# Dealing the later modulation blocks 12 and 8, instead of 10 and 10, to the two attention stages of a two-layer trunk step

## The chip, the core and the metric

The kernel runs on one core of a Trainium2 chip. It is measured in device microseconds of one launch. Before the change the median of three runs is 1972.08 us (1971.47 to 1976.73). About 0.3% (5.9 us) is what a measurement of this kernel can tell from no change.

## What is computed

One step of a two-layer trunk over 128 context tokens and 512 latent tokens of width 1024 (640 tokens in all). Each layer first computes its modulation, six vectors of 1024 for each of two conditions (context and latent), from the conditioning vector and a large matrix. Layer 0 mixes tokens with two kinds of attention, layer 1 with two kinds of recurrence, and each layer ends in a gated convolutional FFN.

```python
def trunk_layer(h, cond, p, mixer, ctx):
    sh1, sc1, g1, sh2, sc2, g2 = jnp.split(jax.nn.silu(cond) @ p['ada_w'] + p['ada_b'], 6, axis=-1)
    hn = rmsnorm(h, p['norm1']) * (1.0 + sc1) + sh1
    m, ctx_out = mixer(hn, p['mix'], ctx)
    h = h + g1 * m
    hn = rmsnorm(h, p['norm2']) * (1.0 + sc2) + sh2
    h = h + g2 * conv_ffn(hn, p)
    return h, ctx_out
...
def one(qblk):
    s = jnp.einsum('bhqd,bhkd->bhqk', qblk, k).astype(jnp.float32) * scale
    p = jax.nn.softmax(s, axis=-1).astype(v.dtype)
    return jnp.einsum('bhqk,bhkd->bhqd', p, v)
```

`ada_w` is 1024 x 6144 in each layer. The differential attention (A) takes two softmax maps per head and query block and subtracts one from the other; the latent attention (B) takes one. Both have four heads. Latent queries see 640 keys, context queries 128.

## The kernel before

All large weights go through one ring of two slots in SBUF. The SyncE queue issues the loads in the order of a list of blocks; a load into a slot waits until the block that lay there two places earlier is released by the matmuls that read it (`released`). A modulation block is 512 columns of `ada_w`, 2048 KB. There are 24 of them, numbered 0 to 23: blocks 0 to 3 (`ADA_FIRST = 4`) are computed at the very start, since layer 0 needs them at once. The other twenty are computed inside the two attention stages, ten in each (`BATCH = 10`): the first stage (A, g = 0) takes blocks 4 to 13 and the second (B, g = 1) blocks 14 to 23.

An attention stage has 20 units, numbered 0 to 19 here: four heads by five query blocks, the fifth of each head being the context queries (units 4, 9, 14, 19, with 128 keys only). In round u, TensorE works through this order (`att_pe`): the scores of unit u; half a modulation block (`products(u)`, so one block in two units); in the rounds of later heads the product of an earlier head's weights with its values (a round with u % 5 == 2 has both a latent and a context product); in the second stage's first five rounds the factor of the sub-norm (`sub_factor`); and the five transposes of unit u-1's probabilities. VectorE takes the maximum and scales the probabilities, ScalarE takes the exponential and copies the transposes out of PSUM. In the first stage the scores of unit u wait for the two exponentials of unit u-1 (`att0_exp`), since both maps share two PSUM places. The transposes of unit u-1 wait for its scaled probabilities (`att0_probs`, `att1_probs`).

The first half of a block begins with a wait for its load (`next_block`: `block_loaded0` or `block_loaded1`, one for each slot), and its second half releases the slot. Everything behind that wait in TensorE's queue waits too. Half a block is four matmuls of a 128 x 32 stationary operand against 128 x 512 columns, each placed in its own 32 output rows of one PSUM bank (the profile shows two records for each, so 8 for a half block). The stationary operand is a window into a row of zeros with the two conditioning columns in it, moved by two columns per block, so that all blocks of a batch add up in one bank. At the end of the stage the bank is copied once, turned (`batch_turn`) and added to the bias (`batch_take_cols`).

Just ahead of the first stage both slots are not alike. Block 4 is loaded long before, but block 5 goes into the slot that the last block of the input projection held until that projection ended. Behind block 23 in the list come the two blocks of the output projection.

Of the kernel before, what the change touches and what calls it, by code (L numbers as in the profile page):

```python
# [19 lines left out]
P = 128  # L20
# [16 lines left out]
EPS = 1e-6  # L37
ADA_FIRST = 4
RING = 2
BATCH = (24 - ADA_FIRST) // 2  # L40
COND0 = 2 * (BATCH - 1)
SLOT = 4096
SEG = ((0, NL), (NL, NT))
# [30 lines left out]
def build(nc, t_in, t_out):  # L74
# [3 lines left out]
    with ctx:  # L78
# [3 lines left out]
        def sem(name):  # L82
            return ctx.enter_context(nc.semaphore(name))
# [3 lines left out]
        def bank(b, n=512, p0=0, p1=P):  # L87
            return ps_all[p0:p1, 512 * b:512 * b + n]
# [49 lines left out]
        def pc(name, i=0, w=1, p0=0, p1=P):  # L138
            return par[p0:p1, PC[name] + i:PC[name] + i + w]
# [54 lines left out]
        def sg(name):  # L194
            if name not in S:
                S[name] = sem(name)
            return S[name]
# [27 lines left out]
        def mm(pe, out, lhsT, rhs, first=True, last=True):  # L225
            return pe.matmul(out, lhsT, rhs, start=first, stop=last)  # L226
# [36 lines left out]
        ada_row = lambda n: stat[:, 512 * (n % 2):512 * (n % 2) + 512]  # L263
        cond = lambda k, b: cond_b[:, COND0 + 32 * k - 2 * b:COND0 + 32 * k - 2 * b + 32]
        group_sum = small[:, 130:130 + 2 * BATCH]
        ada_w = {}

        def ada_products(pe, n, ks):

            g, b = divmod(n - ADA_FIRST, BATCH) if n >= ADA_FIRST else (None, 0)  # L270
            if ks[0] == 0:
                ada_w[n] = next_block(pe)
                if g is not None and b == 0:
                    pe.wait_ge(sg("ada_taken"), ADA_FIRST + g)
            for k in ks:
                p0 = 32 * (k % 4)
                ins = mm(pe, bank(ada_rows_bank(n), 512, p0, p0 + 32), cond(k, b), ada_w[n][:, k, :],
                         k < 4 and b == 0, k >= 4 and b == (0 if g is None else BATCH - 1))
            if ks[-1] == KT - 1:
                ins.then_inc(sg("ada_rows"), 1)  # L280
                released.append((sg("ada_rows"), n + 1))
# [18 lines left out]
                .then_inc(sg("ada_taken"), 1)  # L300

        def batch_take_rows(dve, g):
            dve.wait_ge(sg("ada_rows"), ADA_FIRST + BATCH * (g + 1))
            dve.tensor_copy(ada_row(g), bank(7)).then_inc(sg("ada_rowed"), 1)

        def batch_turn(pe, g):
            pe.wait_ge(sg("ada_rowed"), ADA_FIRST + g + 1)
            for m in range(4):
                ins = mm(pe, bank(7)[:, 32 * m:32 * m + 2 * BATCH], ada_row(g)[:, P * m:P * m + P], group_sum)
            ins.then_inc(sg("ada_cols"), 1)  # L310

        def batch_take_cols(dve, g):

            dve.wait_ge(sg("ada_cols"), ADA_FIRST + g + 1)
            n0 = ADA_FIRST + BATCH * g
            for l in range(2):
                a, b = max(n0, 12 * l), min(n0 + BATCH, 12 * l + 12)
                if a < b:
                    ins = dve.tensor_tensor(
                        mods[:, 8 * a:8 * b].rearrange("p (b m c) -> p b m c", m=4, c=2),  # L320
                        bank(7, P).rearrange("p (m b c) -> p b m c", m=4, c=2)[:, a - n0:b - n0],
                        pc(f"ada_b{l}", 4 * (a - 12 * l), 4 * (b - a)).rearrange("p (b m) -> p b m", m=4).unsqueeze(3)
                        .to_broadcast([P, b - a, 4, 2]), ALU.add)
            ins.then_inc(sg("ada_taken"), 1)
# [959 lines left out]
        def att_units():  # L1284
            return [(hd, qt) for hd in range(4) for qt in range(5)]
# [3 lines left out]
        ROUNDS = 21  # L1289

        latent_at = lambda hd: 2 * hd + 2 if hd < 3 else 7
        context_at = lambda hd: 2 * hd + 1 if hd < 3 else 8

        def att_pe(pe, g):
            maps = 2 - g
            units = att_units()
            x = f"att{g}_"

            def scores(u):
                if u >= len(units):
                    return
                hd, qt = units[u]
                if g == 1 and u < 2:
                    pe.wait_ge(sg("m0_copied"), U0_AT + 11 + u)
                if g == 0:
                    sides = ((0, 0, 64), (1, 64, P))
                    if u >= 1:
                        pe.wait_ge(sg(x + "exp"), 2 * u)  # L1310
                else:
                    sides = ((u % 2, 0, QK),)
                    if u >= 2:
                        pe.wait_ge(sg(x + "exp"), u - 1)
                lhs = lambda p0, p1: q_b[p0:p1, NT * hd + P * qt:NT * hd + P * qt + P]
                key = lambda p0, p1, a, b: k_b[p0:p1, NK * hd + a:NK * hd + b]
                if qt < 4:
                    for pair, p0, p1 in sides:
                        mm(pe, pair_ap(pair, 0, 512), lhs(p0, p1), key(p0, p1, 0, 512))
                    for pair, p0, p1 in sides:  # L1320
                        mm(pe, pair_ap(pair, 512, 640), lhs(p0, p1), key(p0, p1, 512, 640)).then_inc(sg(x + "scores"), 1)
                else:
                    for pair, p0, p1 in sides:
                        mm(pe, pair_ap(pair, 0, P), lhs(p0, p1), key(p0, p1, KP0, NK)).then_inc(sg(x + "scores"), 1)

            def transposes(u):
                if not 0 <= u < len(units):
                    return
                hd, qt = units[u]
                pe.wait_ge(sg(x + "probs"), u + 1)  # L1330
                if u >= 1:
                    pe.wait_ge(sg(x + "turned_out"), u)
                if u >= 6:
                    pe.wait_ge(sg(x + "out"), context_at((u - 1) // 5 - 1))
                pb = pr_b[:, (u % 2) * 2 * NT:(u % 2) * 2 * NT + NT]
                for kt in range(5 if qt < 4 else 1):
                    ins = pe.transpose(bank(4)[:, P * kt:P * kt + P] if kt < 4 else bank(5, P), pb[:, P * kt:P * kt + P],  # L1337
                                       ident[:, :])
                ins.then_inc(sg(x + "turned"), 1)

            def value(hd, kt):
                if kt == 0:
                    pe.wait_ge(sg(x + "turned_out"), 5 * hd + 4)
                    if hd >= 1:
                        pe.wait_ge(sg(x + "out"), latent_at(hd - 1))
                    elif g == 1:
                        pe.wait_ge(sg("sub_scaled"), 5)
                ins = mm(pe, bank(6), v_b[:, 512 * kt + P * hd:512 * kt + P * hd + P],
                         dT_b[:, (hd % 2) * 2560 + 512 * kt:(hd % 2) * 2560 + 512 * kt + 512], kt == 0, kt == 4)
                if kt == 4:  # L1350
                    ins.then_inc(sg(x + "values"), 1)

            def context_value(hd):
                pe.wait_ge(sg(x + "turned_out"), min(5 * hd + 6, 20))
                mm(pe, bank(5)[:, P:2 * P], v_b[:, 512 * 5 + P * hd:512 * 5 + P * hd + P],
                   dTp_b[:, (hd % 2) * P:(hd % 2) * P + P]).then_inc(sg(x + "values"), 1)

            def products(u):
                if 0 <= u < len(units):
                    if g == 1 and u == 0:  # L1360
                        pe.wait_ge(sg("head_root"), 1)
                    ada_products(pe, ADA_FIRST + BATCH * g + u // 2, range(4 * (u % 2), 4 * (u % 2) + 4))

            for u in range(ROUNDS):
                hd, r = u // 5 - 1, u % 5
                scores(u)
                products(u)
                if hd >= 0 and r == 2:
                    context_value(hd)
                if 0 <= hd < 3 and r > 0:  # L1370
                    value(hd, r)
                if g == 1 and hd < 0:
                    sub_factor(pe, r)
                if g == 0 and u == len(units):
                    up0_query(pe, 2)
                    up0_query(pe, 0)
                transposes(u - 1)
                if 0 <= hd < 3 and r == 0:
                    value(hd, 0)
            for kt in range(5):  # L1380
                value(3, kt)
            context_value(3)
# [80 lines left out]
        def att_dve(dve, g, ch):  # L1463
# [58 lines left out]
            if g == 1:  # L1522
                batch_take_cols(dve, 1)
# [804 lines left out]
        for piece in wkv_order():  # L2328
            piece_use[piece] = []
            for _ in range(banks_of.get(piece[0], 0)):  # L2330
                u = len(use_bank)
                b = FIRST_BANKS[u] if u < first_uses else 4 + (u - first_uses) % 3
# [1001 lines left out]
```

## Time and profile before

| | before |
|---|---|
| median of three runs | 1972.08 us (1971.47 to 1976.73) |
| the profiled execution's own time | 1973.24 us |
| its span in the profile | 1971.5 us |
| TensorE matmul busy | 1890.9 us (96%) |
| VectorE, ScalarE, GpSimd busy | 1094.3, 727.9, 139.5 us |
| DMA | 164.20 MB, mean 83 GB/s |
| first attention stage, about | 165 to 252 us |
| second attention stage, about | 268 to 343 us |

The span is one execution of the whole program. Each engine has its own row of busy time; a wait on an engine that is not the one everything else waits for costs nothing. TensorE is the engine to look at here, and the question at each place is whether it works, waits for another engine or waits for a load.

### The profile page before, as it was taken

To read this page: it belongs to the slowest core of one execution; us is meant where nothing else is said; L and a number is where in the kernel's file an instruction comes from. 1 tells how busy PE (TensorE), PEld (TensorE's weight loads), DVE (VectorE), ACT (ScalarE), POOL (GpSimd) and SP (SyncE) were. 2 spreads that over 40 slices of the span, in tenths; PEclk is the share of its full clock that TensorE was granted. 3 is DMA by queue.
4 is the path that set the end of the run, shared out by engine and by line. 5 is a ranking of instruction groups with operands and counts; after the bars stand their busy time and mean duration, and the time that the engine had idled before them with its cause. 6 is when DMAs were issued, how large, how long until landed. Compare 5 with 4: busy or idle time off the path is not lost.

```text
span 1971.5 us, 41405 instructions
## 1 busy us (share of the span) xinstructions
PE 1890.9 (96%) x18391; PEld 1693.8 (86%) x18391; DVE 1094.3 (56%) x2007; ACT 727.9 (37%) x1331; POOL 139.5 (7%) x137
## 2 busy tenths in 40 slices
PE   5998999999999999999999889898999999999997
PEld 2794444999999999999998678788779999999997
DVE  3646744575555562254565766766677554557223
ACT  2324565343332341132245644444324332334211
POOL 2000000000000000000002523322000000000000
PEclk8999999999999999999999899999999999999999
DMA  9125748121222222322221000000212122212322
GB/s 344 56 86 195 275 144 295 43 86 63 67 86 86 70 62 60 89 83 86 64 65 42 7 3 4 4 4 4 92 43 77 53 86 86 83 46 63 86 74 69
DMA packets 142034, 164.20 MB, mean 83 GB/s; under 512 B 2496, under 2 KB 107120, under 8 KB 141856
## 3 DMA queue, kind: packets, MB, share of 16 engines
q1 hardware_dynamic: 138736, 150.29, 23.7%
q0 software_dynamic: 3120, 11.26, 1.6%
q8 instruction: 145, 2.38, 0.5%
q14 instruction: 33, 0.27, 0.0%
HBM read 157.79 MB, written 3.75 MB: 82 GB/s over the span
## 4 chain that ended last, share of the span: by engine, by line
PE 87%; DVE 7%; ACT 2%; POOL 1%; issue 1%; DMA 1%; POOLq 0%; DVEq 0%; SPq 0%; ACTq 0%
PE ps L226 81%; DMA ring<-in_ada_w 1%; PE ps L2485 1%; POOL work L2849 1%; PE ps L1337 1%; DVE work L498 1%; DVE ring L2734 1%; DVE small L1473 1%; PE ps L2090 1%; ACT work L1401 0%; POOL work L2851 0%; PE ps L2463 0%; DVE x_lo_r L504 0%; PE ps L347 0%; PE ps L462 0%
## 5 line engine op out<-in xcount | busy, mean ns | idle before, releaser
L226 PE MATMUL ps<-x_hi_r,w_lo 128*128 128x320 f32 (+2 forms) x2224 | 516.1, 307 | 0.4 <-DVE w_lo L1702 0.4
L226 PE MATMUL ps<-x_hi_r,w_hi 128*128 128x320 f32 (+2 forms) x1792 | 428.7, 311 | 0.9 <-issue 0.9
L226 PE MATMUL ps<-x_lo_r,w_hi 128*128 128x320 f32 (+2 forms) x1792 | 424.8, 308 | 0.0
L226 PEld LDWEIGHTS ps<-x_hi_r,w_lo 128*128 128x128 f32 x2224 | 370.3, 187 | 1.8 <-issue 0.5
L226 PEld LDWEIGHTS ps<-x_lo_r,w_hi 128*128 128x128 f32 x1792 | 305.6, 188 | 0.0
L226 PEld LDWEIGHTS ps<-x_hi_r,w_hi 128*128 128x128 f32 x1792 | 303.8, 188 | 1.4 <-issue 1.3
L226 PE MATMUL ps<-work 64*64 64x64 f32 (+10 forms) x3284 | 269.4, 277 | 18.9 <-ACT work L1401 7.6
L226 PEld LDWEIGHTS ps<-work 64*64 64x64 f32 (+5 forms) x3284 | 173.1, 152 | 93.3 <-issue 59.0
L741 DVE SCALAR_TENSOR_TENSOR work<-ps,par,work 128x511 f32<-128x511 f32 (+1 forms) x188 | 103.4, 550 | 254.8 <-ACT work L908 244.8
L908 ACT ACTIVATE work<-ps,par 128x640 f32<-128x640 f32 x88 | 77.8, 884 | 374.3 <-PE ps L226 374.3
L785 ACT ACTIVATE w_hi<-ring 128x1024 fp32r<-128x1024 f32 (+1 forms) x152 | 135.6, 937 | 206.4 <-DMA ring<-in_ffn_down 183.3
L796 DVE TENSOR_TENSOR w_lo<-ring,w_hi 128x1024 fp32r<-128x1024 f32 (+1 forms) x152 | 158.5, 1077 | 88.9 <-ACT w_hi L785 88.9
L226 PE MATMUL ps<-g_lo,w_hi 128*128 128x320 f32 (+2 forms) x704 | 174.7, 309 | 0.0
L226 PE MATMUL ps<-work,ring 64*64 64x64 f32 (+3 forms) x2368 | 122.1, 238 | 8.1 <-DVE work L2752 4.0
L226 PEld LDWEIGHTS ps<-work,ring 64*64 64x64 f32 (+2 forms) x2368 | 95.0, 142 | 31.7 <-issue 25.9
L226 PEld LDWEIGHTS ps<-g_lo,w_hi 128*128 128x128 f32 x704 | 121.3, 188 | 0.0
L226 PE MATMUL ps<-x_lo_r,w_lo 128*128 128x320 f32 (+2 forms) x416 | 108.2, 310 | 0.0
L743 DVE SCALAR_TENSOR_TENSOR work<-ps,par,work 128x511 f32<-128x511 f32 (+1 forms) x188 | 103.3, 550 | 6.7
L448 DVE SCALAR_TENSOR_TENSOR h<-ps,mods,h 128x512 f32<-128x512 f32 (+2 forms) x76 | 34.8, 493 | 122.0 <-PE ps L226 121.8
L226 PE MATMUL ps<-x_hi_r,w_in_hi 128*128 128x320 f32 (+1 forms) x384 | 88.3, 312 | 0.5 <-issue 0.4
L226 PE MATMUL ps<-x_lo_r,w_in_hi 128*128 128x320 f32 (+1 forms) x384 | 86.8, 307 | 0.0
L226 PE MATMUL ps<-ring,cond 128*32 128x512 f32 x384 | 56.0, 667 | 18.0 <-DMA ring<-in_ada_w 18.0
(407 smaller groups left out, 2591.1 us busy)
## 6 DMA issues: line engine op xcount, KB each, us to landing
ring<-in_ada_w SPq DMA_DIRECT2D x24, 2048.0 KB, 8.2
ring<-in_ffn_up SPq DMA_DIRECT2D x44, 1024.0 KB, 7.7
ring<-in_ffn_down SPq DMA_DIRECT2D x16, 1408.0 KB, 6.9
ring<-in_l_w_in SPq DMA_DIRECT2D x11, 1024.0 KB, 5.2
ring<-in_l_w_out SPq DMA_DIRECT2D x4, 2048.0 KB, 8.5
ring<-in_l_w_in SPq DMA_DIRECT2D x3, 2048.0 KB, 9.7
h<-in_xT POOLq DMA_DIRECT2D x1, 2560.0 KB, 14.8
out_yT<-work POOLq DMA_DIRECT2D x2, 768.0 KB, 4.0
```

The costliest lines, as they stand in the source:

```text
L226: return pe.matmul(out, lhsT, rhs, start=first, stop=last)
L448: ins = dve.scalar_tensor_tensor(h(m, x, y), psum(u % 2, x, y), gate(m, c), h(m, x, y), ALU.mult, ALU.add)
L498: ins = dve.scalar_tensor_tensor(hn(t, x, y), h(t, x, y), gain(t, c), bank(6 + p)[:, x - a:y - a], ALU.mult, ALU.mult)
L741: ch(dve.scalar_tensor_tensor(acc(a + 1, b), psrc(a, b - 1), w0, acc(a + 1, b), ALU.mult, ALU.add))
L743: ins = dve.scalar_tensor_tensor(acc(a, b - 1), psrc(a + 1, b), w2, acc(a, b - 1), ALU.mult, ALU.add)
L785: act.activation(wh_b[:, SLOT * (f % 2) + w * part:SLOT * (f % 2) + w * part + w], ring[:, SLOT * (n % RING) + w * part:SLOT * (n % RING) ...
L796: dve.tensor_tensor(wl_b[:, at:at + w], ring[:, at:at + w], wh_b[:, SLOT * (f % 2) + w * part:SLOT * (f % 2) + w * part + w].bitcast(F32), ...
L908: act.activation(tile(cacc, 2 * (m % 2) + half), spair(n % 3, cut=up_cut(n)), ACT.Identity, bias=pc(f"ffn_b{l}", half * FT + m), scale=cw( ...
L1337: ins = pe.transpose(bank(4)[:, P * kt:P * kt + P] if kt < 4 else bank(5, P), pb[:, P * kt:P * kt + P], ident[:, :])
L1473: dve.tensor_reduce(small[:, c:c + 1], pair_ap(i % 2, 0, w), AXX, ALU.max, negate=True)\
L2090: pe.matmul(out(hd), xtok[:, 512 * c + 64 * hd:512 * c + 64 * hd + 64], M_b[:, 1024 * x + P * hd:1024 * x + P * hd + P], start=hd % 4 < 2, ...
L2485: x = pe.matmul(XB(g)[p0:p1, c - 5 * g, :], XT_(n)[q0:q1, c, :], V_[q0:q1, c, :], start=False, stop=True, skip_group_check=True)
```

## The change

The twenty blocks are now dealt 12 and 8. The first stage takes blocks 4 to 15, the second blocks 16 to 23. The new function `halves_at(g, u)` says which half blocks a unit does: in the first stage's units 0 to 3 two halves each, that is blocks 4, 5, 6 and 7 whole, and in units 4 to 19 one half each (blocks 8 to 15); in the second stage one half in each unit but those with u % 5 == 2 (units 2, 7, 12 and 17), which do none. The row of zeros ahead of the conditioning columns grows from 18 to 22, the sum matrix from 20 to 24 columns, and `batch_turn` writes 24 and 16 columns instead of 20 and 20. The number of half blocks, of loads and their order in the list stay the same.

```diff
-BATCH = (24 - ADA_FIRST) // 2
+BATCHES = (12, 8)
+BATCH = max(BATCHES)
+BATCH_AT = (ADA_FIRST, ADA_FIRST + BATCHES[0])
...
-            g, b = divmod(n - ADA_FIRST, BATCH) if n >= ADA_FIRST else (None, 0)
+            g = None if n < ADA_FIRST else int(n >= BATCH_AT[1])
+            b = 0 if g is None else n - BATCH_AT[g]
...
-                         k < 4 and b == 0, k >= 4 and b == (0 if g is None else BATCH - 1))
+                         k < 4 and b == 0, k >= 4 and b == (0 if g is None else BATCHES[g] - 1))
...
         def batch_take_rows(dve, g):
-            dve.wait_ge(sg("ada_rows"), ADA_FIRST + BATCH * (g + 1))
+            dve.wait_ge(sg("ada_rows"), BATCH_AT[g] + BATCHES[g])
...
-                ins = mm(pe, bank(7)[:, 32 * m:32 * m + 2 * BATCH], ada_row(g)[:, P * m:P * m + P], group_sum)
+                ins = mm(pe, bank(7)[:, 32 * m:32 * m + 2 * BATCHES[g]], ada_row(g)[:, P * m:P * m + P],
+                         group_sum[:, 0:2 * BATCHES[g]])
...
+        def halves_at(g, u):
+            counts = [(2 if v < 4 else 1) if g == 0 else int(v % 5 != 2) for v in range(u + 1)]
+            return sum(counts[:u]), sum(counts)
...
-                    ada_products(pe, ADA_FIRST + BATCH * g + u // 2, range(4 * (u % 2), 4 * (u % 2) + 4))
+                    for i in range(*halves_at(g, u)):
+                        ada_products(pe, BATCH_AT[g] + i // 2, range(4 * (i % 2), 4 * (i % 2) + 4))
```

TensorE in the kernel before, units 0 to 2 of the first attention stage. Rows with `work 128x512` and `128x128 x2` are scores, `ring,cond` the modulation products, L1337 the transposes.

```order
L226 MATMUL ps<-ring,cond 32x512 [waits ada_taken,block_loaded0]
L226 MATMUL ps<-ring,cond 32x512 x3
L226 MATMUL ps<-work 128x512 [waits att0_exp]
L226 MATMUL ps<-work 128x512
L226 MATMUL ps<-work 128x128 x2
L226 MATMUL ps<-ring,cond 32x512 x4
L1337 MATMUL ps<-ident,work 128x128 [waits att0_probs]
L1337 MATMUL ps<-ident,work 128x128 x4
L226 MATMUL ps<-work 128x512 [waits att0_exp]
L226 MATMUL ps<-work 128x512
L226 MATMUL ps<-work 128x128 x2
L226 MATMUL ps<-ring,cond 32x512 [waits block_loaded1]
```

The same place in the changed kernel (the transposes are its L1346).

```order
L228 MATMUL ps<-ring,cond 32x512 [waits ada_taken,block_loaded0]
L228 MATMUL ps<-ring,cond 32x512 x7
L228 MATMUL ps<-work 128x512 [waits att0_exp]
L228 MATMUL ps<-work 128x512
L228 MATMUL ps<-work 128x128 x2
L228 MATMUL ps<-ring,cond 32x512 [waits block_loaded1]
L228 MATMUL ps<-ring,cond 32x512 x7
L1346 MATMUL ps<-ident,work 128x128 [waits att0_probs]
L1346 MATMUL ps<-ident,work 128x128 x4
L228 MATMUL ps<-work 128x512 [waits att0_exp]
L228 MATMUL ps<-work 128x512
L228 MATMUL ps<-work 128x128 x2
```

The wait for block 5 (`block_loaded1`) moved from unit 2 to unit 1, ahead of the transposes of unit 0 and the scores of unit 2. Units 0 and 1 now each begin and end a block, and so do units 2 and 3 behind them.

TensorE in the kernel before, units 1 and 2 of the second attention stage (`sqb,ident` is the sub-norm's factor).

```order
L226 MATMUL ps<-ring,cond 32x512 x4
L226 MATMUL ps<-sqb,ident 128x512 [waits sub_scaled]
L1337 MATMUL ps<-ident,work 128x128 [waits att1_probs]
L1337 MATMUL ps<-ident,work 128x128 x4
L226 MATMUL ps<-work 128x512 [waits att1_exp]
L226 MATMUL ps<-work 128x128
L226 MATMUL ps<-ring,cond 32x512 [waits block_loaded1]
L226 MATMUL ps<-ring,cond 32x512 x3
L226 MATMUL ps<-sqb,ident 128x512 [waits sub_scaled]
L1337 MATMUL ps<-ident,work 128x128 [waits att1_turned_out,att1_probs]
L1337 MATMUL ps<-ident,work 128x128 x4
```

The same place in the changed kernel.

```order
L228 MATMUL ps<-ring,cond 32x512 x4
L228 MATMUL ps<-sqb,ident 128x512 [waits sub_scaled]
L1346 MATMUL ps<-ident,work 128x128 [waits att1_probs]
L1346 MATMUL ps<-ident,work 128x128 x4
L228 MATMUL ps<-work 128x512 [waits att1_exp]
L228 MATMUL ps<-work 128x128
L228 MATMUL ps<-sqb,ident 128x512 [waits sub_scaled]
L1346 MATMUL ps<-ident,work 128x128 [waits att1_turned_out,att1_probs]
L1346 MATMUL ps<-ident,work 128x128 x4
L228 MATMUL ps<-work 128x512 [waits att1_exp]
L228 MATMUL ps<-work 128x128
L228 MATMUL ps<-ring,cond 32x512 [waits block_loaded1]
```

Unit 2 has lost its four products; nothing stands now between its scores and the factor that precedes the transposes of unit 1. Units 7, 12 and 17 lose theirs in the same way.

## Rows read from the trace of the kernel before

**Rows 1.** The page: TensorE's total, its clock in 40 slices, the engines' chain.

```profile
PE 1890.9 (96%) x18391; PEld 1693.8 (86%) x18391; DVE 1094.3 (56%) x2007; ACT 727.9 (37%) x1331; POOL 139.5 (7%) x137
...
PEclk8999999999999999999999899999999999999999
...
PE 87%; DVE 7%; ACT 2%; POOL 1%; issue 1%; DMA 1%; POOLq 0%; DVEq 0%; SPq 0%; ACTq 0%
```

**Rows 2.** Busy time by stretch: first attention stage (two), second stage; with granted clock.

```profile
core 0: us, PE busy (x) PEld busy (x) DVE busy (x) ACT busy (x) POOL busy (x), PEclk, DMA share, GB/s
...
170.00:180.00 10.00, 8.18 (x62) 3.65 (x59) 8.93 (x17) 5.06 (x13) 0.00 (x0) 1.00 0.96 338
...
190.00:200.00 10.00, 9.48 (x55) 4.49 (x55) 8.07 (x17) 6.27 (x17) 0.00 (x0) 1.00 0.84 299
270.00:280.00 10.00, 10.00 (x52) 4.38 (x52) 6.20 (x12) 3.69 (x11) 0.00 (x0) 1.00 0.60 210
```

**Rows 3.** TensorE in order of time, first attention stage, units 0, 1, 2, 4 and 6.

```profile
166.61 1.06 PE L226 MATMUL ps<-ring,cond 128*32 128x512 f32 x8
169.41 1.35 PE L226 MATMUL ps<-work 64*128 64x512 f32 x8 [1.74 <-ACT work L1401]
170.69 1.07 PE L226 MATMUL ps<-ring,cond 128*32 128x512 f32 x8
171.69 0.77 PE L1337 MATMUL ps<-ident,work 128*128 128x128 f32 x5
173.37 1.35 PE L226 MATMUL ps<-work 64*128 64x512 f32 x8 [0.91 <-ACT work L1401]
174.65 1.06 PE L226 MATMUL ps<-ring,cond 128*32 128x512 f32 x8
...
181.69 1.07 PE L226 MATMUL ps<-ring,cond 128*32 128x512 f32 x8
...
188.86 1.06 PE L226 MATMUL ps<-ring,cond 128*32 128x512 f32 x8
```

**Rows 4.** SyncE in order of time: when the loads of blocks 5 and 6 were issued.

```profile
164.64 0.37 SPq L3169 DMA_DIRECT2D ring<-in_ada_w  x1
...
171.82 0.37 SPq L3169 DMA_DIRECT2D ring<-in_ada_w  x1
```

**Rows 5.** DMA issues from 164 to 166, and all modulation loads; last column issue to landing.

```profile
ring<-in_ada_w SPq DMA_DIRECT2D x1, 2048.0 KB, 9.6
out_k<-work POOLq DMA_DIRECT2D x1, 256.0 KB, 7.1
...
ring<-in_ada_w SPq DMA_DIRECT2D x24, 2048.0 KB, 8.2
```

**Rows 6.** TensorE, second attention stage, units 2 and 7.

```profile
275.12 1.07 PE L226 MATMUL ps<-ring,cond 128*32 128x512 f32 x8
...
277.08 0.71 PE L1337 MATMUL ps<-ident,work 128*128 128x128 f32 x5
...
292.60 1.06 PE L226 MATMUL ps<-ring,cond 128*32 128x512 f32 x8
...
294.78 0.71 PE L1337 MATMUL ps<-ident,work 128*128 128x128 f32 x5
```

**Rows 7.** VectorE in the same two units: the scaling of the probabilities.

```profile
276.15 0.55 DVE L1486 TENSOR_SCALAR work<-work,small 128x640 f32<-128x640 f32 x1
...
293.63 0.55 DVE L1486 TENSOR_SCALAR work<-work,small 128x640 f32<-128x640 f32 x1
```

**Rows 8.** Busy time by stretch around waits of TensorE elsewhere (columns as Rows 2).

```profile
43.00:49.00 6.00, 4.91 (x9) 2.70 (x10) 6.00 (x14) 6.00 (x13) 4.44 (x8) 0.50 1.04 392
1131.50:1134.50 3.00, 0.60 (x8) 0.31 (x3) 2.63 (x4) 1.63 (x4) 2.53 (x2) 1.00 0.00 0
1135.00:1138.00 3.00, 3.00 (x94) 2.75 (x94) 1.75 (x4) 0.74 (x2) 0.00 (x0) 0.50 0.03 5
1343.00:1350.00 7.00, 4.10 (x174) 3.51 (x170) 6.56 (x16) 2.11 (x5) 1.91 (x2) 1.00 0.01 2
```

More of the change, by code:

```diff
@@ L314, in batch_take_cols @@
             dve.wait_ge(sg("ada_cols"), ADA_FIRST + g + 1)
-            n0 = ADA_FIRST + BATCH * g
+            n0 = BATCH_AT[g]
             for l in range(2):
-                a, b = max(n0, 12 * l), min(n0 + BATCH, 12 * l + 12)
+                a, b = max(n0, 12 * l), min(n0 + BATCHES[g], 12 * l + 12)
                 if a < b:
```

## The prediction

> **What bounds the kernel now.** I read the page first: TensorE has matmuls for 96% of the span, and the chain that ended last lies on it for 87% [rows 1]. So a microsecond of TensorE work or waiting is a microsecond of time, unless the trace shows slack where it falls. The chain's small shares of VectorE (7%) and ScalarE (2%) say that slack exists somewhere, so next I looked at the busy time by stretch in the two attention stages, the only places the change touches. In the first stage from 170 to 180 us, TensorE is busy for 8.18 of 10 us and VectorE for 8.93; from 190 on, when the value products have joined, TensorE is at 9.48. In the second stage it is at 10.00 [rows 2]. The same rows have a column that speaks of something else: the DMA engines are busy for 0.96 of 170 to 180. This stage runs at the pace at which modulation blocks arrive, or near it, and one has to look at each load.
>
> So third, the order of time. In units 0 to 4 of the first stage TensorE does scores (1.35), half a block (1.06), transposes (0.77), and then waits for ScalarE: 1.74 us once, then 0.91 in a unit; units begin 4 us apart [rows 3]. Fourth, the loads. Block 5's was issued at 164.64, when the input projection let go of its slot, and took 9.6 us to land, more than the median of 8.2, since stores such as that of `out_k` run beside it [rows 4, 5]. It lands at 164.64 + 9.6 = 174.2. Its first product starts at 174.65 in unit 2 [rows 3]. That is 0.4 us of slack. Block 6 is issued at 171.82, when unit 1 has finished block 4; with 8.2 it lands at 180, for a product at 181.69. The kernel before takes its blocks just in time.
>
> **What is removed: four half blocks from the second stage.** Units 2, 7, 12 and 17 lose one half block each, 1.0 us of TensorE (the next instruction begins that much behind it). If TensorE alone set the pace this would give 4 x 1.0 = 4.0 us. But the transposes behind it wait for the probabilities. In unit 2 VectorE scales them from 276.15 to 276.70, after a maximum that needs this unit's scores, which don't move. The transposes start at 277.08; they can come forward only to about 276.75, which gives 0.33 us. In unit 7 the scaling ends at 293.63 + 0.55 = 294.18, and the transposes at 294.78 can come to about 294.23: 0.55 us [rows 6, 7]. Units 12 and 17 are built like unit 7. Sum: 0.33 + 3 x 0.55 = 1.98, say 2.0 us. Bounds: 1.0, if half of that is lost to something I don't see, and 4.0. I take 2.0, since it is read from the very units. What is late next is VectorE's scaling.
>
> **What is added: four half blocks in the first stage's units 0 to 3.** By TensorE alone they would be almost free. Each costs 1.0 us, and the waits for ScalarE in these units are 1.74 and 0.91 [rows 3]; what sticks out is 0.1 us in each of three units. The price comes from the loads.
>
> Unit 0 now does all of block 4 (166.6 to 168.7), so the load of block 6 is issued at 168.7. Unit 1 needs block 5 at 170.7, and it lands at 174.2, because its issue hangs on the input projection and not on this stage. TensorE stands for 3.5 us; behind the waiting product, the transposes of unit 0 and the scores of unit 2 are queued, and through these VectorE and ScalarE too.
>
> From then on loads follow each other without a pause. A block is 2.097 MB; at the 392 GB/s of a stretch in which the DMA engines were full [rows 8] that is 5.4 us. The earliest landings of blocks 6, 7 and 8 are thus 174.2 + 5.4 = 179.6, then 185.0, then 190.4. A block can't land before issue + 8.2 either. At the full clock: block 5's products 174.2 to 176.3 (block 7 issued), transposes and scores to 178.4, block 6's products 179.6 to 181.7 (block 8 issued), transposes and scores to 183.7, block 7's products 185.0 to 187.1, transposes and the short scores of unit 4 to 188.2, and block 8's first half at the later of 181.7 + 8.2 and 190.4, so at 190.4. It replaces the product at 181.69 before [rows 3]: 8.7 us late. From unit 4 on, a unit does half a block again, as before, and each load has more time than before: block 9, issued at 187.1, lands by 195.8, and is wanted at 188.86 + 8.7 = 197.6. So the lag grows no more. It isn't won back either: TensorE is at 9.48 of 10 there [rows 2], and the chain runs over it.
>
> **The clock.** TensorE's granted clock is 1.00 in these stretches [rows 2]. Elsewhere in this trace a stretch with 0.60 us of matmuls in 3 is followed by a stretch at 0.50 (1.2 GHz) of some 3 us, and before 49 us one of 6 us at 0.50 is seen; but 4.10 busy in 7 us kept 1.00 [rows 8]. A wait of 3.5 us, with only the scores of unit 1 (1.35 us) between it and the idle time before them, is much more like the former. The Trainium skill (TensorE: Matmul & The Clock Gate, "Why this matters for your kernels") warns of just this: gaps without matmuls between bursts send the clock back to half. The rows on the fall agree with it.
>
> I reckon with a low clock over 4.8 of the 5.3 us between 174.2 and 179.6 (between the 3 and the 6 us of the rows). Work then takes twice as long, and 2.4 us are lost: block 5's products end at 178.4 (block 7 issued, landing at 186.6), unit 2's scores at 180.8, and block 6's products at 182.8. Block 7's run 186.6 to 188.7, and block 8 lands 5.4 behind block 7, at 192.0. The lag is 192.0 - 181.69 = 10.3 us. So the fall costs only 1.6 us, because the loads hide the rest.
>
> **Small edits at nothing.** The wider row of zeros and the sum matrix are set at the start, behind loads that TensorE waits for anyway; `batch_turn` has 4 columns more in one stage and 4 fewer in the other; the vectors that `batch_take_cols` adds stay two in the first stage. In the second stage, the output projection's first block is issued a unit earlier, which no one waits for.
>
> **The sum.** +10.3 - 2.0 = +8.3 us. The profiled execution took 1973.24 us and its span 1971.5; it would become 1981.5. It lies 1.2 above the median of three, 1972.08, which becomes 1980.4. That is slower by 0.42%.
>
> **Rivals.**
> - *The loads pace it, but the clock stays at 1.00.* For it: the waits of 1.74 and 0.91 us did nothing. Against: this one is twice as long, and little is done just ahead of it. 8.7 - 2.0 = +6.7: 1978.8.
> - *More than one fall, or loads that share.* The waits before blocks 7 and 8 are still 1.7 to 2.2 us (184.9 to 186.6, and 189.8 to 192.0), and a fall behind unit 4 meets a stage with no slack: 3 us at half the clock lose 1.5 each. Or block 6's load, issued 3 us earlier, takes bandwidth from block 5's: together they land at 179.6 all the same, but block 5 some 3 us later (177.4), block 7 is issued at 179.5, and blocks 7 and 8 move on to about 193.2, a lag of 11.5. The Trainium skill (DMA: Bandwidth & Descriptors, "Queues, rings and completion order") says that each DMA engine takes the descriptors of one ring in their order, which speaks for block 5 landing first; no row here shows two modulation loads issued so close in this stage. Either way +9.5 to +12.5: 1981.6 to 1984.6.
> - *Faster: block 5 arrives without being waited for, and the added halves vanish in the waits for ScalarE.* It decides at one place, the product of block 5 in unit 1: were the block there by 170.7 (a load of 6.1 us), and blocks 6 to 8 in their turn, the first stage would pay 3 x 0.1 us. The second would give 2.0 to 4.0, and the time would be 1968.4 to 1970.4. Against it: 9.6 us is this very load in the trace, and nothing in the change issues it earlier.
> - *A wash.* The landings come 1 to 2 us earlier each than I think (the stores are over by 175 us), and TensorE's halves of the second stage count in full: 8.7 - 1.0 - 4.0 = +3.7: 1975.8.
>
> **Chances.** Forecast 0.47; clock at 1.00 0.18; more falls or shared loads 0.18; a wash 0.12; faster 0.05. The first three lie above +5.9 us (0.3%), but the second so closely that I give a sixth of it to no change. So faster 0.05, within 0.3% 0.15, slower 0.80. The range runs from 1976.6, which leaves out the faster case and most of the wash, to 1984.4; it leaves out about 0.2.
>
> **What would show it.** In the profile after: in unit 1 the products start 3 to 4 us behind the scores' end, with the DMA `ring<-in_ada_w` as the releaser; before units 2, 3 and 4 there are further waits of 1 to 2 us on the same; products of unit 4 lie at about 190 to 192, and from there to the stage's end the order of time is that of before plus 9 to 10.5. The granted clock shows 0.5 somewhere from 172 to 182. In the second stage, units 2, 7, 12 and 17 are shorter by 0.3 to 0.6 and not by 1.0, their transposes released by VectorE's L1486 (in its new place). I am wrong if block 5 lands before 172, if TensorE goes on through units 0 to 3 without a wait for DMA, or if the lag shrinks between unit 5 and the end of the first stage.

## The result, and the profile after

The changed kernel takes 1986.07 us (median of 5 runs, 1983.69 to 1993.89) against 1972.08 us (median of 5, 1969.07 to 1976.73). The ratio is 1.0071, with a 95% interval from 1.0057 to 1.0085: slower by 11.2 to 16.8 us. The forecast was slower, by 8.3 us, with a range up to 1984.4 us; the direction was right and the time lies above the range. Three later series of the same kernel gave ratios of 1.0054 (1.0033 to 1.0075), 1.0061 (1.0044 to 1.0079) and 1.0057 (1.0038 to 1.0077). All its 23 runs together have a mean of 1985.7 us, and the 58 of the kernel before that ran beside one or another of these series or experiments one of 1973.7 us, 12.0 us less.

The profiled execution was the shortest of the first five, 1983.69 us with a span of 1981.9 us. Two places of the page show the change. In the chain the DMA has 2% now where it had 1%, GpSimd 2% where it had 1%, and TensorE 85% instead of 87%. In the costliest groups, the modulation products (all 24 blocks) wait for their loads for 28.0 us now and for 18.0 before (the number behind the second bar; the last row is that of before).

```profile
PE 85%; DVE 7%; DMA 2%; POOL 2%; ACT 2%; issue 1%; POOLq 0%; DVEq 0%; SPq 0%; ACTq 0%
...
L228 PE MATMUL ps<-ring,cond 128*32 128x512 f32 x384 | 56.9, 686 | 28.0 <-DMA ring<-in_ada_w 28.0
...
L226 PE MATMUL ps<-ring,cond 128*32 128x512 f32 x384 | 56.0, 667 | 18.0 <-DMA ring<-in_ada_w 18.0
```

TensorE in order of time through units 0 to 5 of the first stage answers to [rows 3]. In brackets stands the idle time and what ended it.

```profile
162.99 1.35 PE L228 MATMUL ps<-work 64*128 64x512 f32 x8 [0.72 <-ACTq L207]
164.27 1.92 PE L228 MATMUL ps<-ring,cond 128*32 128x512 f32 x16
167.07 1.35 PE L228 MATMUL ps<-work 64*128 64x512 f32 x8 [0.88 <-ACT work L1411]
172.20 3.64 PE L228 MATMUL ps<-ring,cond 128*32 128x512 f32 x16 [3.77 <-DMA ring<-in_ada_w]
175.77 1.03 PE L1346 MATMUL ps<-ident,work 128*128 128x128 f32 x5
176.74 1.35 PE L228 MATMUL ps<-work 64*128 64x512 f32 x8
178.01 1.92 PE L228 MATMUL ps<-ring,cond 128*32 128x512 f32 x16
...
183.84 1.92 PE L228 MATMUL ps<-ring,cond 128*32 128x512 f32 x16 [1.79 <-DMA ring<-in_ada_w]
185.69 0.77 PE L1346 MATMUL ps<-ident,work 128*128 128x128 f32 x5
186.39 0.49 PE L228 MATMUL ps<-work 64*128 64x128 f32 x4
190.39 1.93 PE L228 MATMUL ps<-ring,cond 128*32 128x512 f32 x8 [3.51 <-DMA ring<-in_ada_w]
192.25 1.32 PE L1346 MATMUL ps<-ident,work 128*128 128x128 f32 x5
193.50 1.35 PE L228 MATMUL ps<-work 64*128 64x512 f32 x8
```

The stage begins 2.34 us earlier here than in the profile before (162.99 against 165.33), so only differences within the stage can be compared. Three of the forecast waits are there: 3.77 us in unit 1 for block 5, 1.79 in unit 3 for block 7 and 3.51 in unit 4 for block 8, all ended by a modulation load. One should also look at how long the products take. Sixteen of them take 1.92 us in unit 2 and 3.64 in unit 1; eight take 1.93 us in unit 4, where eight took 1.07 before. Those are the two spells at half the clock, which the busy time by stretch shows (columns as in [rows 2]):

```profile
168.00:170.00 2.00, 0.42 (x6) 0.19 (x2) 1.88 (x3) 0.69 (x1) 0.00 (x0) 0.89 1.03 396
170.00:176.00 6.00, 3.80 (x17) 0.83 (x18) 1.93 (x6) 0.98 (x4) 0.00 (x0) 0.50 1.05 398
176.00:190.00 14.00, 9.03 (x67) 4.13 (x66) 8.48 (x21) 6.41 (x18) 0.00 (x0) 0.99 0.98 350
...
190.00:194.00 4.00, 3.61 (x15) 1.43 (x17) 0.00 (x0) 0.39 (x1) 0.00 (x0) 0.57 1.03 381
```

SyncE's queue gives the loads. Block 6 is issued at 166.26, block 7 only at 175.90, behind the slow products of unit 1, and block 8 at 180.00; the column at the end of the second fence is issue to landing, for blocks 6, 7 and 8 in this order. They land at 177.5, 183.8 and 190.3.

```profile
166.26 0.37 SPq L3179 DMA_DIRECT2D ring<-in_ada_w  x1
...
175.90 0.37 SPq L3179 DMA_DIRECT2D ring<-in_ada_w  x1
```

```profile
ring<-in_ada_w SPq DMA_DIRECT2D x1, 2048.0 KB, 11.2
...
ring<-in_ada_w SPq DMA_DIRECT2D x1, 2048.0 KB, 7.9
...
ring<-in_ada_w SPq DMA_DIRECT2D x1, 2048.0 KB, 10.3
```

In the second stage, units 2 and 7 answer to [rows 6]. Unit 2's products are gone, and its transposes now wait for VectorE's scaling (L1496, L1486 before):

```profile
284.92 1.02 PE L228 MATMUL ps<-sqb,ident 128*128 128x512 f32 x2
286.66 0.77 PE L1346 MATMUL ps<-ident,work 128*128 128x128 f32 x5 [0.72 <-DVE work L1496]
...
303.88 0.77 PE L1346 MATMUL ps<-ident,work 128*128 128x128 f32 x5 [0.45 <-DVE work L1496]
```

Where the time went can be read from four marks in TensorE's order: the first scores of the first stage, the first product of the second, and the first matmul of the output projection behind it.

| | before | changed, four profiles |
|---|---|---|
| first scores to first product of the second stage | 102.98 us | 115.21, 116.14, 116.83, 116.94 |
| from there to the output projection | 74.96 us | 73.27, 73.27, 73.29, 73.26 |
| all the rest of the span | 1793.6 us | 1793.4, 1797.6, 1793.2, 1797.0 |
| first scores to unit 4's first product | 16.36 us | 27.40, 27.17, 27.87, 27.96 |

The first stage lost 13.3 us in the mean, the second gave 1.7. That is +11.6 us, against 12.0 in the means over all runs. The column of before is one profile; that its first stage takes 102.98 us is borne out by two experiments below, with 102.98 and 103.32.

### The profile page after: what moved, and what is told of

It is laid out like the page before. It is cut to its first block, busy times and chain, and to the rows that moved or that the text cites. A ratio compares the mean times of both kernels' runs of the same rounds, so it can differ in the third digit from the quotient of the medians.

```text
span 1981.9 us, 41405 instructions
## 1 busy us (share of the span) xinstructions
PE 1894.1 (96%) x18391; PEld 1695.4 (86%) x18391; DVE 1094.4 (55%) x2007; ACT 729.0 (37%) x1331; POOL 139.7 (7%) x137
## 4 chain that ended last, share of the span: by engine, by line
PE 85%; DVE 7%; DMA 2%; POOL 2%; ACT 2%; issue 1%; POOLq 0%; DVEq 0%; SPq 0%; ACTq 0%
PE ps L228 80%; DMA ring<-in_ada_w 2%; POOL work L2859 1%; PE ps L2495 1%; PE ps L1346 1%; DVE ring L2744 1%; DVE work L502 1%; DVE small L1483 1%; POOL work L2861 1%; PE ps L2100 1%; PE ps L2473 0%; DVE x_lo_r L508 0%; PE ps L466 0%; DVE work L2762 0%; DVE work L2757 0%
```

## The experiments

**Are the loads the price, or the moved work?** Blocks 5 to 8 are loaded with one eighth of their bytes, and every product of theirs reads that piece. Their modulation values are left out; the instructions of the engines are the same.

```diff
+                if 12 * l + b in (5, 6, 7, 8):
+                    blocks.append(("ada", [(t_in[f"ada_w_{l}"][0:P, 512 * b:512 * b + 512]
+                                            .rearrange("(k p) c -> p k c", p=P), 1, 0, 512, 512)]))
+                    return
...
-                ins = mm(pe, bank(...), cond(k, b), ada_w[n][:, k, :],
+                ins = mm(pe, bank(...), cond(k, b), ada_w[n][:, 0 if n in (5, 6, 7, 8) else k, :],
```

> The changed kernel with blocks 5 to 8 cut to one eighth of their bytes (256 KB instead of 2048 KB); their products all read that one piece, so the same instructions run and those blocks' modulation values are left out. Theory A (the first stage's loss is waiting for the loads of blocks 5 to 8): no wait of TensorE on a modulation load in units 0 to 4; from the first scores of the first stage to the first product of the second stage 103.3 us, against 103.0 before and 115.2 in the changed kernel; with 1.7 us gained in the second stage the whole is 1.4 us under the kernel before, about 1970.7 us. Rival B (the moved work itself costs, 4 half blocks on a TensorE with little slack): the stretch takes about 107 us and the whole is 2 us or more above the kernel before.

Measured: no wait for a load in these units, and 102.98 us in the first stage, the same as before to the hundredth, though four more half blocks are in it. The second stage takes 73.27. The ratio is 0.9996 (0.9984 to 1.0008). In its order of time, the transposes of unit 0 begin 1.85 us behind the start of unit 1's products, and the scores of unit 2 come at 174.29, 3.95 us behind those of unit 1:

```profile
170.34 1.35 PE L231 MATMUL ps<-work 64*128 64x512 f32 x8 [0.88 <-ACT work L1414]
171.62 1.92 PE L231 MATMUL ps<-ring,cond 128*32 128x512 f32 x16
173.47 0.76 PE L1349 MATMUL ps<-ident,work 128*128 128x128 f32 x5
174.29 1.35 PE L231 MATMUL ps<-work 64*128 64x512 f32 x8
```

In [rows 3] units 1 and 2 are 3.96 us apart as well. The moved work costs nothing that the profile shows, and the interval ends at 1.6 us above the kernel before; rival B falls. The whole loss of the first stage hangs on the bytes of four loads.

**What does the second stage give by itself?** The first stage is dealt 10 blocks as before, the second 8; blocks 22 and 23 are left out.

```diff
-BATCHES = (12, 8)
+BATCHES = (10, 8)
...
-                    for n in range(ADA_FIRST, 24):
+                    for n in range(ADA_FIRST, 22):
...
-            counts = [(2 if v < 4 else 1) if g == 0 else int(v % 5 != 2) for v in range(u + 1)]
+            counts = [1 if g == 0 else int(v % 5 != 2) for v in range(u + 1)]
...
+            ch(dve.memset(mods[:, 8 * 22:8 * 24], 0.0))
```

> The changed kernel with the first stage as before (10 blocks, half a block in each unit) and 8 blocks in the second stage, so that blocks 22 and 23 are neither loaded nor computed (their modulation values are left out). It shows the second stage's gain alone. Theory A (VectorE's scaling is late next): units 2, 7, 12, 17 are shorter by 0.3 and 3 x 0.5 us, 1.7 us in all, the first stage is that of before, and the whole is 1.7 us under the kernel before, about 1970.4 us: within what can be told from no change. Rival B (TensorE alone sets the pace): 4.0 us less, 1968.1 us.

Measured: first stage 103.32 us (with one wait of 0.52 us for block 6 in unit 4), second stage 73.28, that is 1.7 us less than before. The ratio is 1.0003 (0.999 to 1.0015). The profile carries theory A. The whole can't tell 1.7 us from nothing, but its interval ends at 2.0 us below the kernel before, so rival B's 4.0 are excluded. The wait for block 6 shows how close the old schedule is: in the trace of before this load, issued at 171.82 [rows 4], took

```profile
ring<-in_ada_w SPq DMA_DIRECT2D x1, 2048.0 KB, 9.5
```

and landed at 181.3, for a product at 181.69 [rows 3]. The prediction reckoned with the median of 8.2 here; the slack is 0.4 us, as for block 5.

**Is it the place of the blocks or their number?** Twelve blocks in the first stage still, but with their halves placed by the loads.

```diff
-            counts = [(2 if v < 4 else 1) if g == 0 else int(v % 5 != 2) for v in range(u + 1)]
+            counts = [{0: 2, 1: 0, 2: 2, 8: 2, 13: 2, 18: 2}.get(v, 1) if g == 0 else int(v % 5 != 2)
+                      for v in range(u + 1)]
```

> The same deal of 12 and 8 blocks, but the halves of the first stage placed by the loads: unit 0 does block 4 whole, unit 1 none, unit 2 block 5 whole, then one half a unit, and two in units 8, 13 and 18. Theory A (the place of the moved blocks costs, not their number): no wait for block 5; a wait of 1 us for block 6 in unit 3 and up to 1.5 us behind each later double; the stretch from the first scores to the second stage's first product 106 to 108 us instead of 115.2, the whole 1.5 to 3.5 us over the kernel before, 1973.6 to 1975.6. Rival B (the number of moved blocks costs; the ring can't carry 12 blocks in this stage): 112 us or more and 1981 us or more.

Measured: 107.43 us in the first stage, 73.27 in the second, 1976.34 us (12 runs), ratio 1.0011 (0.9999 to 1.0024). Four short waits for loads are left, the three shown and one of 0.29 us:

```profile
181.97 1.06 PE L228 MATMUL ps<-ring,cond 128*32 128x512 f32 x8 [1.16 <-DMA ring<-in_ada_w]
...
208.96 1.07 PE L228 MATMUL ps<-ring,cond 128*32 128x512 f32 x8 [1.48 <-DMA ring<-in_ada_w]
...
230.18 1.07 PE L228 MATMUL ps<-ring,cond 128*32 128x512 f32 x8 [1.37 <-DMA ring<-in_ada_w]
```

The same deal of 12 and 8 thus costs 4.5 us in the first stage instead of 13.3. That is in theory A's range and under rival B's 112. Eight or nine of the thirteen microseconds are the place of the whole blocks, the falls of the clock among them, since the granted clock is 1.00 from 166 to 196 here. Even so nothing is won over the kernel before.

**Is block 5's late start the whole cause?** Only block 5 is made small (its values are left out); the edit is that of the first experiment with `(5,)` in place of the four.

> The changed kernel with block 5 alone cut to one eighth of its bytes, so that it lands before unit 1 wants it (its modulation values are left out). Theory F (block 5's late start is the whole cause): no further waits, the stretch 103 to 104 us and the kernel 0 to 1 us under the one before. Theory A (the ring has no lead for four whole blocks in four units, whenever it starts): waits of 2 to 4 us for blocks 6, 7 and 8 in units 2 to 4, the product of unit 4 some 6.6 us later than before, the stretch 109.5 to 111.5 us, the kernel 5 to 7.5 us above the one before, 0.25 to 0.4%.

Measured: 110.76 us in the first stage, 1980.88 us (12 runs), ratio 1.0036 (1.0021 to 1.0051). Theory F falls. Block 5 is there in time, and the waits move one place on:

```profile
180.11 1.92 PE L231 MATMUL ps<-ring,cond 128*32 128x512 f32 x16 [1.82 <-DMA ring<-in_ada_w]
...
186.52 1.92 PE L231 MATMUL ps<-ring,cond 128*32 128x512 f32 x16 [2.51 <-DMA ring<-in_ada_w]
...
191.88 1.94 PE L231 MATMUL ps<-ring,cond 128*32 128x512 f32 x8 [2.32 <-DMA ring<-in_ada_w]
```

So this ring of two slots doesn't feed four blocks to four units even when the first of them is there in time. And the last row, eight products in 1.94 us, shows the clock falling here too. It didn't fall in the longer wait of 2.51 us (184.0 to 186.5), but in the next one of 2.32 us (189.6 to 191.9), as the clock, the third number from the end, shows:

```profile
185.00:186.00 1.00, 0.00 (x0) 0.00 (x0) 0.76 (x2) 1.00 (x3) 0.00 (x0) 1.00 0.90 283
...
191.00:192.00 1.00, 0.12 (x4) 0.12 (x8) 0.51 (x2) 0.00 (x0) 0.00 (x0) 0.74 1.02 377
192.00:193.00 1.00, 1.00 (x8) 0.08 (x8) 0.00 (x0) 0.00 (x0) 0.00 (x0) 0.50 1.08 406
```

Ahead of the first of these waits TensorE worked for 3.9 us, ahead of the second for 3.0 us. The length of a wait alone doesn't decide.

**What do the falls of the clock cost?** Matmuls of no use fill most of the waits.

```diff
                 if 0 <= u < len(units):
+                    for _ in range({1: 3, 3: 1, 4: 2}.get(u, 0) if g == 0 else 0):
+                        mm(pe, bank(6), ident[:, :], h(0, 0, 512))
                     for i in range(*halves_at(g, u)):
```

> The changed kernel with matmuls of no use (128x128 by 128x512, into a free PSUM bank, about 1 us each at full clock) in front of the products: three in unit 1, one in unit 3, two in unit 4, where TensorE otherwise waits for a load. It shows what the falls of the clock cost. Theory C (the falls cost 2 to 3 us, since products at half the clock issue the next load later and delay the unit behind them): granted clock 1.00 from 165 to 195, the stretch from the first scores to the second stage's first product 112.5 to 113.5 us instead of 115.2, and a median of 1982 to 1984 against 1986.1, with less spread. Theory A alone (the loads set the pace and hide the falls): 115 us and 1986 us. Rival D: the added matmuls run into the landing and cost time of their own: 116 us or more.

> The changed kernel with the useless matmuls in units 1, 3 and 4 once more, beside the changed kernel on one chip. Theory C: the stretch 112.8 us as in the first profile of it, and a median 1.5 to 4 us below the changed kernel's. Rival: no difference, which would leave the fall of the clock without a price in the whole.

> The changed kernel with the useless matmuls a third time, beside the changed kernel on one chip. In the profiles the stretch is 112.9 us against 116.1, but the whole so far differs by under 1 us between the two. Theory C: the stretch 112.9 us again and, over all runs of both, the changed kernel 1.5 to 3.5 us slower in the mean. Rival G: the stretch is 112.9 but the whole does not differ, since low clock elsewhere (before the first stage, or in the scans) takes back what is saved; the sum of what lies before and behind the two stages would be 3 us more than in the changed kernel's profiles.

Measured in the three profiles: 112.84, 112.87 and 112.96 us in the first stage, with the clock at 1.00 all through. The waits for loads are still there, behind the fillers:

```profile
166.00:196.00 30.00, 23.96 (x145) 9.51 (x145) 15.45 (x35) 10.70 (x28) 2.35 (x4) 1.00 0.97 353
```

```profile
176.55 1.93 PE L228 MATMUL ps<-ring,cond 128*32 128x512 f32 x16 [0.98 <-DMA ring<-in_ada_w]
...
181.95 1.92 PE L228 MATMUL ps<-ring,cond 128*32 128x512 f32 x16 [1.49 <-DMA ring<-in_ada_w]
...
187.37 1.92 PE L228 MATMUL ps<-ring,cond 128*32 128x512 f32 x16 [0.47 <-DMA ring<-in_ada_w]
...
193.82 1.07 PE L228 MATMUL ps<-ring,cond 128*32 128x512 f32 x8 [1.50 <-DMA ring<-in_ada_w]
```

This splits the first stage's 13.3 us: 112.9 - 102.98 = 9.9 us is the pace of the loads at full clock, and 116.3 - 112.9 = 3.4 us the two falls. Of these, 1.1 us are there by unit 4's product (a lag of 11.2 us in the mean, and of 10.1 with fillers) and 2.3 come behind it. In the stretch, theory C holds. In the whole it isn't shown. The medians were 1985.83, 1985.29 and 1981.95 us; the first is above the 1982 to 1984 that was expected, and the second 0.3 to 0.6 us below the changed kernel's two series beside it instead of 1.5 to 4; only the third, 2.8 us below the series beside it, is as expected. All 19 runs have a mean of 1984.7 us, 1.0 us (+-2.1) below the 23 of the changed kernel, where the profiles of the stretch give 3.4. What lies before and behind the two stages is 1797.0, 1797.2 and 1794.4 us in the filled kernel's profiles and 1793.2 to 1797.6 in the changed kernel's. It varies by more than the difference that is asked for (1793.0 to 1797.8 over all twelve profiles of this case), and rival G is neither shown nor excluded.

**Do the falls come at the same places each time?** The changed kernel, three times more.

> The changed kernel once more, for the time against the kernel before on this chip and for a second profile with the clock's falls at other places. Theory A+C (loads of blocks 5 to 8 pace the first stage, and the falls add 1.5 to 4 us by where they come): first scores to the second stage's first product 113 to 118 us (115.2 in the first profile), second stage 73.3 us, median 10 to 15 us above the kernel before. Rival E (something behind the attention stages also got longer): the stretch from the end of the second stage to the end of the program is 3 us or more above the 1628 to 1631 us seen so far.

> The same kernel a third time, for a third profile. The waits in units 1, 3 and 4 are the same in each to within 2 us; the stretch between the stages' markers lies between 113 and 118 us; the spread is by the number and place of the stretches at half the clock.

> The changed kernel a fourth time. Three profiles so far gave 115.2, 116.1 and 116.8 us from the first scores to the second stage's first product, each with two spells at half the clock, one in the wait of unit 1 and one from the wait of unit 4 on. Theory C (two falls at about these places whenever the kernel runs): again two spells and 115 to 117 us. Rival: a profile without the second fall, about 113 to 114 us.

Measured: 1985.87, 1985.63 and 1984.77 us, and the four profiles of the table above. Each has two spells, one in unit 1 and one from the end of unit 4's wait on. The first profile, on which one would build, is the mildest. In it the second spell lasts some 3.5 us and ends with the transposes (1.32 us). In the others it lasts 6.5 to 7. It also covers the scores of unit 5 there, as in the fourth profile:

```profile
194.98 1.93 PE L228 MATMUL ps<-ring,cond 128*32 128x512 f32 x8 [3.93 <-DMA ring<-in_ada_w]
196.85 1.33 PE L1346 MATMUL ps<-ident,work 128*128 128x128 f32 x5
198.11 2.51 PE L228 MATMUL ps<-work 64*128 64x512 f32 x8
```

Scores of 2.51 us instead of 1.35 stand in a stage with little slack: in these three profiles the lag grows by 2.3 to 2.4 us behind unit 4's product, and by 1.2 in the first. Rival E falls: from the output projection's first matmul to the end it is 1626.1 to 1630.4 us in the four profiles, and 1628.2 before.

## Why the prediction went wrong

- *What bounds the kernel, and that block 5 would be waited for*: right. The wait is 3.7 to 3.8 us in four profiles (forecast 3.5), and the further waits are in units 3 and 4. The wait in unit 2 that the text named among the signs did not come; block 6 was there when unit 2 wanted it, since the products of unit 1, at half the clock, had held unit 2 up (so did the working with a fall have it). With fillers, at full clock, a wait of 1.5 us does stand in unit 2.
- *That the added half blocks cost next to nothing by themselves*: right, and shown; with small loads the stage is 102.98 us.
- *The second stage gives 2.0 us, not 4.0, because VectorE's scaling is late next*: right, 1.7 us in every profile, with L1496 as the releaser. In unit 7 the forecast was 0.55, and the unit is shorter by 3.90 - 3.42 = 0.48; in unit 2 it was 0.33, and the unit is shorter by 3.68 - 3.42 = 0.26.
- *The lag at unit 4's product, 10.3 us*: 11.2 in the mean (10.8 to 11.6). At full clock the forecast was 8.7, and with fillers it is 10.1. The mis-sized term is the spacing of the loads, 5.4 us each. With fillers the products of blocks 5, 6 and 7 begin at 176.55, 181.95 and 187.37, 5.4 us apart as reckoned, but those of block 8 at 193.82, 6.45 behind. In the changed kernel block 8's begin 6.4 to 7.1 us behind block 7's. Why this load takes longer no run shows.
- *"The lag grows no more" from unit 4 on*: this is the step that failed. The sum has one fall of the clock, and the wait in front of block 8 brings a second one, in all four profiles. From unit 4's product to the end of the stage the lag grows by 1.2, 2.3, 2.4 and 2.4 us, from 11.2 to 13.3 in the mean; with fillers, where the clock stays up, it shrinks by 0.2. The prediction named this as a rival ("a fall behind unit 4 meets a stage with no slack") and gave it, together with the shared loads, 0.18. Its own rows didn't decide it: it had worked out a wait of 2.2 us before block 8 with 3.2 us of work ahead, and [rows 8] has one stretch of little work with a fall behind it and one of 4.10 us in 7 without. But the 2.2 us hung on the spacing of 5.4. With the measured spacing the wait is 3.4 to 4.1 us, as long as the one in unit 1 from which the prediction did expect a fall. Whether 2.2 us would have brought one at this place no run shows; with block 5 small, 2.32 us did.
- *Loads that share the bandwidth*: this rival has a lag of 11.5 us, near the measured 11.2, but not by its mechanism. It wanted block 5 some 3 us later for block 6's load beside it. Block 5 took 9.8 to 9.9 us from issue to landing in the four profiles, with block 6 issued 4 us behind it, and 9.6 before.
- *One fall costs 1.6 us, since the loads hide the rest*: right in kind, somewhat too high. The first fall costs 1.1 us at unit 4's product, as the fillers show.

The miss has these parts: +0.9 at unit 4's product, +2.1 behind it, where the second fall lies, and +0.3 in the second stage's gain. 8.3 + 3.3 = 11.6 us, which is what the profiles show. The first comparison's 14.0 us is 2.4 above that. No profile shows this rest; its interval begins at 11.2, and the three later series, at 10.6 to 12.0, don't repeat it, so it is taken as the spread of the runs. That the falls carry 3.4 us rests on the profiles of the stretch alone, as said above.

## What to carry to other kernels

Before work is moved into a unit's idle time, look at what the work has to be fed: here the instructions fit, but each half block is tied to half of a 2048 KB load, and the loads landed 0.4 us ahead of use. When a wait is added, ask at every wait of the new schedule, not only at the longest, what a fall of the clock behind it would cost, and price the last one as if nothing hides it, since behind it nothing does. A wait that is the difference of a load's spacing and the work beside it moves by the whole error of the spacing: 5.4 us instead of 6.4 to 7.1 made 2.2 us out of 3.4 to 4.1. A step at which the schedule returns to its old pace is no proof that the lag is over.

## What the runs showed of the hardware

- Loads of 2048 KB, each issued before the one ahead of it had landed, landed 5.2 to 7.2 us apart in the four profiles of the changed kernel. How long one took went with how early it was issued: block 6, issued 5.9 us before block 5 landed, took 11.1 to 11.2 us; block 8, issued 3.6 to 4.2 us before block 7 landed, 10.3 to 10.9; block 7, issued 1.6 to 1.7 us before block 6 landed, 7.9 to 8.1, about what a load alone takes here (block 4, 7.7 to 8.3 us).
- In the first profile the granted clock falls within the wait: it is 0.89 from 168 to 170, inside an idle time that began at 168.4, and 0.50 from 170 to 176, so it stays low for 4 us behind the return of work at 172.2. Waits of 1.7 to 2.2 us in unit 3, between bursts of work, brought no fall in the four profiles of the changed kernel. With block 5 small, a wait of 2.51 us with 3.9 us of work ahead brought none, and the next one, of 2.32 us with 3.0 us of work ahead, did.
- TensorE busy for 23.96 of 30 us in the first profile with fillers, in pieces with waits for loads of up to 1.5 us, kept 1.00.
